# Two transformer blocks on one core: the second layer's attention taken two heads at a time, with query/key blocks between the pairs

## The reference, cut to what matters

```python
h = rms_norm(x, norm1_g)
q, k, v, glu_a, glu_b = split(h @ w_in)        # 3 x 512 and 2 x 512 columns
q = rms_norm(q per head of 64, q_norm_g); k = rms_norm(k per head, k_norm_g)
# 8 heads, stick-breaking attention, s < t
z = q . k / sqrt(64)
w[t,s] = exp(log_sigmoid(z[t,s]) + sum over s<j<t of log_sigmoid(-z[t,j]))
attn = w @ v
c = glu_a * sigmoid(glu_b)                      # 512 channels
c = causal_depthwise_conv(c, 31 taps) + b
c = silu(layer_norm(c over the 512 channels))
x = x + concat(attn, c) @ w_out
```

## Time and profile before

| | |
|---|---|
| Median of 3 runs (lowest, highest) | 1292.04 us (1288.03, 1292.2) |
| The profiled execution | 1293.05 us, span 1291.3 us |
| TensorE busy | 1258.5 us (97%) |
| VectorE, ScalarE, POOL busy | 609.3 us (47%), 495.7 us (38%), 527.5 us (41%) |
| Mean granted TensorE clock | 0.984 of full speed |
| DMA | 118.40 MB, mean 92 GB/s |

### The profile page before, as it was taken

How to read it: one execution, slowest core, us unless ns; L and a number is a source line. 1 busy time by engine, 2 the same in 40 slices (tenths; PEclk the granted TensorE clock), 3 DMA queues, 4 the chain that set the end, 5 groups by cost and what they waited for, 6 DMA issues and landing times.

```text
span 1291.3 us, 16174 instructions
## 1 busy us (share of the span) xinstructions
PE 1258.5 (97%) x5590; PEld 1019.5 (79%) x5590; DVE 609.3 (47%) x882; ACT 495.7 (38%) x655; POOL 527.5 (41%) x244
## 2 busy tenths in 40 slices
PE   8889999999999999999999989899999999999999
PEld 6878888778888888888878766567888888888887
DVE  8893333343653155415564767675443313331332
ACT  6313452234443244314462244556533313332331
POOL 4654553223445344534454433000544453435343
PEclk9889999999999999999999999889999999999999
DMA  7333332112323222322232221000323232223222
GB/s 285 117 128 98 102 112 97 49 49 82 98 97 114 83 97 97 99 97 85 68 126 97 85 95 54 12 1 1 129 83 97 82 121 91 97 82 114 94 73 78
DMA packets 34033, 118.40 MB, mean 92 GB/s; under 512 B 4032, under 2 KB 4160, under 8 KB 33856
## 3 DMA queue, kind: packets, MB, share of 16 engines
q1 hardware_dynamic: 33696, 117.49, 27.4%
q10 hardware_dynamic: 288, 0.24, 0.1%
HBM read 115.61 MB, written 2.10 MB: 91 GB/s over the span
## 4 chain that ended last, share of the span: by engine, by line
PE 89%; DVE 6%; ACT 2%; issue 2%; DMA 1%; POOL 0%; SPq 0%; ACTq 0%; DVEq 0%; POOLq 0%
PE ps L1122 26%; PE ps L1124 26%; PE ps L1123 26%; PE ps L1429 2%; PE ps L1412 1%; PE ps L1287 1%; DVE slab L853 1%; PE ps L1309 1%; PE ps L1456 1%; ACT xg_hi L441 1%; DVE ps L736 1%; DMA h<-x_t 1%; PE ps L1179 1%; PE ps L1180 1%; PE ps L1181 1%
## 5 line engine op out<-in xcount | busy, mean ns | idle before, releaser
L339 POOL TENSOR_TENSOR w_lo<-w_raw,w_hi 128x1024 fp32r<-128x1024 f32 x215 | 517.2, 2409 | 736.3 <-ACT w_hi L425 373.8
L1122 PE MATMUL ps<-xg_hi,w_hi 128*128 128x512 f32 x960 | 380.1, 396 | 10.8 <-DVE slab L668 5.2
L1123 PE MATMUL ps<-xg_lo,w_hi 128*128 128x512 f32 x960 | 375.7, 391 | 0.0
L1124 PE MATMUL ps<-xg_hi,w_lo 128*128 128x512 f32 x960 | 375.6, 391 | 0.0
L1122 PE MATMUL ps<-y_hi,w_hi 128*128 128x512 f32 (+1 forms) x608 | 232.3, 382 | 0.0
L1124 PE MATMUL ps<-y_hi,w_lo 128*128 128x512 f32 (+1 forms) x608 | 230.6, 379 | 0.0
L1123 PE MATMUL ps<-y_lo,w_hi 128*128 128x512 f32 (+1 forms) x608 | 230.5, 379 | 0.0
L1122 PEld LDWEIGHTS ps<-xg_hi,w_hi 128*128 128x128 f32 x960 | 181.8, 189 | 50.8 <-issue 6.8
L1123 PEld LDWEIGHTS ps<-xg_lo,w_hi 128*128 128x128 f32 x960 | 181.8, 189 | 38.5 <-issue 1.4
L1124 PEld LDWEIGHTS ps<-xg_hi,w_lo 128*128 128x128 f32 x960 | 181.5, 189 | 38.2
L425 ACT ACTIVATE w_hi<-w_raw 128x1024 fp32r<-128x1024 f32 x124 | 130.4, 1052 | 126.4 <-PE ps L1124 126.4
(11 more groups left out here) (194 smaller groups left out, 1077.8 us busy)
## 6 DMA issues: line engine op xcount, KB each, us to landing
w_raw<-weights SPq DMA_DIRECT2D x199, 512.0 KB, 3.3
w_raw<-weights SPq DMA_DIRECT2D x16, 384.0 KB, 2.9
out_t<-h SPq DMA_DIRECT2D x8, 256.0 KB, 2.0
h<-x_t SPq DMA_DIRECT2D x3, 512.0 KB, 9.4
slab<-mem_t SPq DMA_DIRECT2D x2, 512.0 KB, 11.1
slab<-mats_in SPq DMA_DIRECT2D x1, 1024.0 KB, 5.3
w_raw<-weights SPq DMA_DIRECT2D x2, 256.0 KB, 3.9
h<-x_t SPq DMA_DIRECT2D x2, 256.0 KB, 4.8
```

Of the source, the lines that this page charges most:

```text
L339: nc.gpsimd.tensor_tensor(w_lo[:, s, :], w_raw[:, s, :], w_hi[:, s, :].bitcast(F32), ALU.subtract).then_inc(w_lo_ready, 1)
L1122: pe.matmul(out, w[0], x[0], start=first, stop=False)
L1123: pe.matmul(out, w[0], x[1], start=False, stop=False)
L1124: return pe.matmul(out, w[1], x[0], start=False, stop=last)
```

## The change: what it does

- **Heads by pairs.** `s_scores(hd)` becomes `pair_scores(j)`: the four score matmuls of head 2j and of head 2j+1 alternate (rows 0 to 63 and 64 to 127 of the array, banks 0 to 2 and 3 to 5), then both heads' masks. ScalarE's logs of both heads, VectorE's sums of both, and both cumulations follow as pairs.
- **Query/key blocks between the pairs.** Only blocks 0 to 3 stand before the first pair. Block 4 comes after the first pair's scores, blocks 5 and 6 after the second pair's, block 7 after the third pair's. Their banks and their waits are new (`qk_block`).
- **The convolution's taps.** All 60 taps of tiles 0 and 1 (in PSUM) are called during the gated unit and the value blocks; at their two ends seven taps of one tile follow each other. The 60 taps of tiles 2 and 3 stand in the query/key and attention part. ScalarE moves tiles 0 and 1 right after, ahead of the first squares.
- **Channel totals on POOL.** POOL adds the four tiles (three additions of 128 x 512) once for the mean and once for the variance, and TensorE sums over the partitions by one matmul each.
- **Halves of `w_lo`.** In the whole kernel POOL splits each weight block by two instructions of 512 columns, each with a semaphore; TensorE waits for the first at a block's begin and for the second ahead of the fifth row tile.
- `final_norm` (eight instructions, L1007) stands as one run behind `ln_centre`. One head's buffer and `wide` become parts of a longer `squares`.

The core of the diff:

```diff
-        QK_BANK = (4, 5, 3, 4, 6, 7, 6, 7)
-        QK_SUM_BANK = (0, 1, 2, 5, 3, 4, 6, 7)
+        QK_BANK = (4, 5, 6, 7, 6, 6, 7, 7)
+        VALUE_BANK = (7, 6, 6, 6)
+        LN_BANK = 7
...
             def weights_lo(b, s):
                 pool.wait_ge(w_hi_ready, b + 1)
-                nc.gpsimd.tensor_tensor(w_lo[:, s, :], w_raw[:, s, :], w_hi[:, s, :].bitcast(F32),
-                                        ALU.subtract).then_inc(w_lo_ready, 1)
+                for half, done in ((slice(0, BLK // 2), w_lo_half), (slice(BLK // 2, BLK), w_lo_ready)):
+                    nc.gpsimd.tensor_tensor(w_lo[:, s, half], w_raw[:, s, half], w_hi[:, s, half].bitcast(F32),
+                                            ALU.subtract).then_inc(done, 1)
...
+            def channel_total(n, tiles, ready):
+                for i in range(1, 4):
+                    ready(i)
+                    if i > 1:
+                        pool.wait_ge(ln_added, 2 * n + i - 1)
+                    nc.gpsimd.tensor_tensor(ln_total, tiles[:, 0, :] if i == 1 else ln_total, tiles[:, i, :],
+                                            ALU.add).then_inc(ln_added if i < 3 else ln_total_ready, 1)
+
+            pool.wait_ge(conv_moved, 2)
+            pool.wait_ge(qk_sums, 8)
+            channel_total(0, conv, lambda i: pool.wait_ge(ln_sum, (2 if i == 1 else 4) * (TAPS - 1)))
+            pool.wait_ge(ln_sums, 1)
+            channel_total(1, conv_in, lambda i: pool.wait_ge(ln_square, i + 1))
...
# ScalarE
+            qk_squares_of(0)
+            qk_squares_of(1)
+            qk_rstd_of(0)
+            qk_squares_of(2)
+            qk_rstd_of(1)
+            qk_squares_of(3)
+            qk_rstd_of(2)
+
+            s_logs(0)
+            s_logs(1)
+            qk_squares_of(4)
+            qk_rstd_of(3)
+            s_weights(0)
+            s_weights(1)
+            qk_rstd_of(4)
...
# VectorE
-                conv_taps((0, 0, 4, 4)[i])
+                conv_taps((0, 4, 5, 5)[i])
...
-                conv_taps((0, 5, 5, 5)[i])
-            conv_taps(23)
+                conv_taps((3, 5, 5, 33)[i])
...
+            qk_input(3)
+            conv_taps(2)
+            qk_apply(2)
+            conv_taps(6)
+
+            s_softplus(0)
+            qk_input(4)
+            s_softplus(1)
+            qk_apply(3)
+            conv_taps(5)
+            qk_apply(4)
+            conv_taps(6)
...
# TensorE
+            def qk_block(t):
+
+                if t < 2:
+                    pe.wait_ge(banks_freed, V2 - USE_LAG)
+                elif t < 4:
+                    pe.wait_ge(conv_moved, 2)
+                elif t == 6:
+                    pe.wait_ge(y_lo_ready, Y_MIX2 + 1)
+                else:
+                    pe.wait_ge(qk_ready, {4: 3, 5: 5, 7: 7}[t])
+                features(QK + t, 0, t % RING, xg, bank=QK_BANK[t], behind=0)
...
                 for tile in (0, 1, 3, 2):
                     bank, at, n = TILES[tile]
+                    if j >= 1 and tile < 2:
+                        pe.wait_ge(s_att, 2 * (2 * j - 1) + tile + 1)
+                    for hd in heads:
+                        r = slice(HD * (hd % 2), HD * (hd % 2) + HD)
+                        pe.matmul(ps[:, 3 * (hd % 2) + bank, at:at + n], k2[r, j, tile * P:(tile + 1) * P],
+                                  q2[r, j, tile * P:], start=tile != 3, stop=False, skip_group_check=True)
...
+            pair_scores(0)
+            qk_block(4)
+            qk_sum(3)
+            s_cumulate(0)
+            s_cumulate(1)
+            qk_sum(4)
+
+            pair_scores(1)
+            pair_values(0)
+            qk_block(5)
+            qk_block(6)
+            qk_sum(5)
+            s_cumulate(2)
+            s_cumulate(3)
+            qk_sum(6)
+
+            pair_scores(2)
+            pair_values(1)
+            qk_block(7)
+            s_cumulate(4)
+            qk_sum(7)
+            s_cumulate(5)
+
+            pair_scores(3)
+            pair_values(2)
+            s_cumulate(6)
+            ln_channel_sums(0)
+            s_cumulate(7)
             pe.wait_ge(s_att, 2 * 6 + 2)
+            output2(0, (0, 1, 2), begin=True)
+            pair_values(3)
+            ln_channel_sums(1)
             output2(1, (0, 1, 2), begin=True)
```

More of the change, by code:

```diff
@@ new lines, in _ @@
+            qk_rstd_of(5)
+            s_weights(2)
+            s_weights(3)
+            qk_rstd_of(6)
+            s_logs(4)
+            pair_values_hi(1)
+            s_logs(5)
+            qk_squares_of(7)
+            s_weights(4)
+            qk_rstd_of(7)
+            s_weights(5)
+            s_logs(6)
+            pair_values_hi(2)
+            s_logs(7)
+            s_weights(6)
+            for i in range(4):
+                act.wait_ge(ln_xc, i + 1)
+                nc.scalar.activation(conv_in[:, i, :], conv[:, i, :], ACT.Square).then_inc(ln_square, 1)
@@ L1070, in s_softplus, with qk_input @@
                                         ALU.add).then_inc(s_sp, 1)
-            for t in range(8):
+            def qk_input(t):
                 multiply_by_rstd((q2, k2)[t % 2][:, t // 2, :], QK + t, QK_BANK[t]).then_inc(banks_freed, 1)
[L1074 to L1079, removed]
             def ln_centre():
@@ L1139, in features @@
                 for n, k in enumerate(order):
+                    if k >= DT // 2 and (n == 0 or order[n - 1] < DT // 2):
+                        pe.wait_ge(w_lo_ready, b + 1)
                     if ready is not None:
@@ L1421, in s_cumulate @@
+                for hd in heads:
+                    for tile in (0, 1, 3, 2):
+                        bank, at, n = TILES[tile]
+                        mm = pe.matmul(ps[:, 3 * (hd % 2) + bank, at:at + P], ident_r[:], far_below_r[:], start=False, stop=False,
+                                       skip_group_check=True)
+                    mm.then_inc(s_z, 1)
             def s_cumulate(hd):
@@ L1473, in ln_channel_sums @@
-                mm.then_inc(ln_sums, 1)
-            for t in range(8):
-                if t == 4:
-                    pe.wait_ge(conv_moved, 2)
-                features(QK + t, QK + t - USE_LAG, t % RING, xg, bank=QK_BANK[t], behind=(5, 6, 3, 3, 0, 0, 2, 2)[t])
-                if t >= 1:
-                    qk_sum(t - 1)
-                if t == 5:
-                    s_scores(0)
+                pe.wait_ge(ln_total_ready, n + 1)
+                pe.wait_ge(*((qk_ready, 8), (ln_xc, 4))[n])
@@ L1485, in output2 @@
+                pe.matmul(ps[:, LN_BANK, :], neg_ones[:], ln_total, start=True, stop=True).then_inc(ln_sums, 1)
             def output2(m, ks, begin=False, end=False):
                 features(WOUT2 + m, WOUT2 + m - USE_LAG, m % RING, yy, ready=y_ready(Y_MIX2), order=ks, begin=begin, end=end)
-            for hd in range(HEADS):
-                if hd + 1 < HEADS:
-                    s_scores(hd + 1)
-                else:
-                    pe.wait_ge(s_att, 2 * 6 + 1)
-                    output2(0, (0, 1), begin=True)
-                s_cumulate(hd)
-                if hd == 0:
-                    qk_sum(7)
-                if hd % 2 == 0 and hd >= 2:
-                    pair_values(hd // 2 - 1)
-                if hd in (5, 7):
-                    ln_channel_sums((hd - 5) // 2)
```

185 lines of the change are left out of this document (91 added, 94 removed).

## The result

The changed kernel takes 1252.24 us (median of 4 runs, 1249.52 to 1253.81) against 1290.38 us for the kernel before (4 runs beside them, 1288.03 to 1292.2): ratio 0.9703, 95% interval [0.9675, 0.9732], 38.1 us less. The profiled execution of after took 1253.81 us (span 1252.1, clock 0.994), 39.2 less than the profiled one of before (1293.05).

What follows compares the result with a forecast made beforehand. TensorE, busy in 97% of the span, was taken as the bound. The profiled 1293.05 us less 26.1 in the stretch and 0.8 elsewhere gave 1266.2; as the profile stood 1.0 above the median, 1265 us, range 1256 to 1276.

Steps and rivals of the forecast that it cites:

- The halves of `w_lo` elsewhere: Outside the stretch, halves gain nothing except at TensorE's wait for the `wide` copy, 37.7 to 41.3 us: 0.8 us.
- The stretch: From the first query/key block's start (742.9 us) to the first finished output block (897.9): 128.9 against 155.0, 26.1 less.
- Scores: A head pair's scores on alternating row halves overlap: 2.5 us, plus 1.2 for masks, four times; 8.8 us less.
- Channel sums: On TensorE in the stretch, eight matmuls become two: 5.2 us less; POOL's additions take 3.6 us a total.
- Waits: TensorE's in the stretch: 2.2 before query/key block 4, 0.6 for head 0's sums, 3.3 for head 6's, 0.1: 6.2 us.
- Clock: Low TensorE clock after the stretch's waits of 2.2 and 3.3 us: 3.0 us for both, bounds 0 and 9.
- Rest: Short waits and restarts of TensorE in the stretch, kept from the old account: 1.8 us.
- VectorE behind POOL: From 745.7 to 846.5 us VectorE stands 17.6 us behind POOL, at 2.2 us for each weight block.
- B: Row halves don't run together in the scores: 2.2 us more per pair, three counting, about 1272; chance 0.12.
- C: VectorE becomes the bound from 745.7 to 846.5 us, at 4.4 us per weight block behind POOL: 1273; chance 0.15.
- D: Slower than before: clock stays at 0.50 from 771 to about 850 us, giving 1332; chance 0.04.
- E: Better than forecast: no fall of the clock and the start gains 2 us, 1262 down to 1257; chance 0.09.

Runs made afterwards that it cites:

- experiment 1: The kernel before with only `w_lo` made in two halves, and TensorE's two waits for them: 1281.25 us, ratio 0.9935.
- experiment 2: The changed kernel with each `w_lo` made by one whole POOL instruction again: 1262.69 us, ratio 0.9796.
- experiment 3: The changed kernel with halves kept, but TensorE waiting for the second half before it begins a block (block 0 excepted): 1250.16 us, ratio 0.9691.
- experiment 4: The changed kernel with the score matmuls of a pair's first head all ahead of the second head's: 1255.02 us, ratio 0.9721.
- experiment 6: The changed kernel with halves for blocks 1 to 27 only, whole instructions after, TensorE waiting for the whole `w_lo`: 1251.71 us, ratio 0.9698.
- experiment 5: The changed kernel with `w_lo` in quarters for blocks 1 to 27, halves after that: 1249.38 us, ratio 0.9683.
- experiment 8: The changed kernel with all eight query/key blocks ahead of the first pair: 1275.62 us, ratio 0.989.
- experiment 10: The changed kernel with the mean's channel sum ahead of head 6's cumulation and taps moved in VectorE's list, halves kept: 1249.62 us, ratio 0.9678.
- experiment 9: The changed kernel with the mean's channel sum earlier, taps moved in VectorE's list, and quarters of `w_lo` in blocks 1 to 27: 1248.92 us, ratio 0.9669.

## Why the prediction was wrong in its time

**The step that failed: "The halves of `w_lo` elsewhere".** It said that between blocks nobody waits for `w_lo`, "so neither gain nor loss", that "One place gains", and "I take 0.8", with bounds of -0.5 and 2. Measured: 10.5 us in the profiles of before and after, and by medians 9.5 (experiment 1) and 10.4 (experiment 2). The mechanism had been read in the earlier trace rows, and applied to that one copy. But it holds for VectorE's copies, tensor-tensor and tensor-scalar instructions whose inputs lie in SBUF, and in the first 97 us VectorE is nearly full: seventeen of its instructions, that copy among them, stood there behind POOL for 1.3 to 2.2 us each, and behind halves none for more than 1.15. The prediction had looked for who waits for `w_lo`, not for who waits while `w_lo` is made; the page's slices show DVE at 8 and 9 in the first three slices, TensorE at 8, and that was the sign to open them. It also left out that a wait of TensorE in the front can bring a low clock, 5.4 us there before and 1.7 after. With 9 to 10 us more for this step the forecast would have been 1255 to 1256, and with the 2.6 us that the stretch gave beyond it about 1253, against 1252.24.

The Trainium skill (SBUF — State Buffer, "Who interferes with whom") has the rule: the one that issues first holds the shared interface for its whole instruction, and the other stands still. The traces agree, with stops of up to 2.2 us behind an instruction of 2.4 and up to 1.15 behind one of 1.3. The prediction cited it for the taps in the stretch only, as an argument against the change, and not for the front, where it speaks for it.

**The stretch, term by term.** Its mechanism was right, and its sizes nearly. TensorE's work: 117.9 forecast. After's 126.4 less 6.6 of waits and 1.7 of clock is 118.1. *Scores* 2.5 and 1.2: measured 2.43 and 1.11 (with overlaps of the spans). *Channel sums* 0.86: 0.86 and 1.05. *Waits* 6.2: 3.7 + 2.1 + 0.8 = 6.6; before block 4 2.2 forecast and 2.1 measured, before head 6's cumulation 3.3 and 3.7. The forecast 0.6 for head 0's sums did not come (VectorE had them at 768.9, TensorE asked at 770.4); the 0.8 ahead of the fourth pair's scores, forecast as 0.1, did: three taps before apply 7 took 4.01 us instead of 2.0, behind two halves and POOL's first addition. *Clock* 3.0: measured 1.7, and there luck had a part, since experiment 3 lost 4.4 behind the same waits. *Rest* 1.8: 0.2 was left. Together 128.9 against 126.4. *VectorE behind POOL* 17.6: the fourteen longest stops in after's stretch, none over 1.1 us and three of them in `final_norm`, add up to 11.5.

**POOL.** A half was taken at 1.2 us: mean 1.31 (430 of them, 554.2 us), minimum 1.26. A total was taken at 3.6. The second took 1.27 + 3.26 us:

```profile
840.13 1.27 POOL L411 TENSOR_TENSOR squares<-slab 128x512 f32<-128x512 f32 x1 [7.86 <-ACT slab L686]
841.54 3.26 POOL L411 TENSOR_TENSOR squares<-squares,slab 128x512 f32<-128x512 f32 x2
```

It ended at 844.8; the matmul that needs it came at 845.9: no wait.

**The rivals.** B fell (experiment 4). C fell as a bound, though its mechanism is alive: every wait left in the stretch ends on VectorE, and experiments 2 and 6 (whole instructions) have three waits for sums there instead of one. D fell: the low level lasted 3.4 us in one place. E, "better", was right in its sign, at 0.09 chance, but its low end of 1257 lies 5 us above the result: it allowed the start 2 us and no fall of the clock, and there was one.

**What stays open.** The same lists give different fronts. With halves in it the first pooling matmul came at 82.4 to 87.3 us (eight profiles), with whole instructions at 97.64 (before) and 89.12 (experiment 2). After's profile is one with a late front (2.9 us of wait at the slab), which may be why experiments 3 and 5 look 2 to 3 us faster. Which VectorE instruction falls behind which half differs from one profile to the next, and what decides it was not tried. Two parts of the change were not undone alone: the new order of the convolution's taps, which took away the 3.7 us wait for bank 6, and `final_norm` as one run.

## What to carry to other kernels

Where VectorE is near full, an instruction on POOL costs VectorE up to nearly its whole length each time it meets a copy, tensor-tensor or tensor-scalar instruction whose inputs lie in SBUF. So cut long POOL instructions into pieces, even if nobody waits for their results; here two pieces gave 9.5 to 10.4 us, and four gave nothing more that could be measured. Before costing an edit that touches the whole kernel, go through each stretch for the engine that is full there, not only through the stretch that the change is about. And put independent blocks of TensorE's work between the links of a long chain on other engines: it saves the waits, and low clock besides (experiment 8: 14.4 us and 9.3).

## What the runs showed of the hardware

- A POOL subtraction of 128 x 1024 took 2.34 us at least and 2.41 on average, one of 128 x 512 1.26 and 1.31: two halves cost 0.2 us more than a whole. All halves together cost 554.2 us of POOL against 517.2 in before, 37 us more that nobody waits for.
- A VectorE addition over 16 columns took 0.17 us alone, 2.25 behind a whole POOL instruction and 1.15 behind a half. A copy with one SBUF input (`wide`) stood behind POOL as well: 2.56 and 1.51 us. Instructions with an input in PSUM did not (at most 0.02 us).
- Sixteen float32 score passes with 64 rows each took 2.43 us with the row halves alternating, and 4.04 with one head after the other.
- Falls of the clock followed TensorE waits of 1.9 us (experiment 10, at head 1's cumulation: 5.43 instead of 3.75 us) and 2.1 us (after); in experiment 9 the same wait of 1.9 us had none. After the same wait of 3.7 us the cumulation of head 6 took 3.75 us in after and experiment 5, and 6.43, 5.17 and 5.30 us in experiments 3, 2 and 6. The length of one wait does not tell whether the clock falls.
